# A hybrid decoder step on one core: the samples' state products turned on TensorE and summed in groups by VectorE

## The chip, the cores and the metric

The kernel runs on one core of a Trainium2 chip. The metric is the time of one launch on the device in microseconds (us); a time is compared as the median of several runs. The engines are named as in the profile: PE is TensorE's matrix multiplication and PEld its loading of stationary weights, DVE is VectorE, ACT is ScalarE, POOL is GpSimd, and SP is SyncE, which issues most DMAs.

## The reference, cut to what matters

One layer of a decoder is computed for a prompt of 16 learned + 256 tokens and for 8 samples of one token each. RMSNorm, a wide input projection, a short convolution branch, an mLSTM branch with 8 heads, an output projection, then a gated feed-forward part with a convolution, and a last RMSNorm. Model width is 2048, a head has 128 key and 256 value columns. For a sample the mLSTM step of one head is

```
c_new = carry * c_prev + g * k v^T          # 128 x 256 state per sample and head
num   = q . c_new                           # sum over the 128 key rows
den   = q . n_new
h     = num / max(|den|, exp(-m))
```

What is edited is the sum `q . c_new`: for each of the 8 samples, 256 numbers, each a sum over 128 key rows.

## The kernel before, in words

The activations lie with features on the 128 partitions and tokens along the free axis (prompt columns first, the 8 samples as the last 8 columns). All weights are streamed from memory once in units of 128 x 1024 float32. For each unit SP loads `w_raw` (a ring of 4), ACT rounds it to `w_hi` (L713), DVE subtracts to `w_lo` (L984), and PE runs three passes of 8 matmuls: `w_hi` with the high part of the activations (L1526), `w_hi` with their low part (L1530), `w_lo` with the high part (L1534). Two units make a strip, one 128-row block of outputs in one of four PSUM banks. PE takes the units in a fixed written order; before each unit it waits for `hi_done`, before the third pass for `lo_done`. DVE makes `w_lo` four units ahead: its `step(i)` in a head makes the low part of unit i + 4. The next load into a `w_raw` slot waits for the `w_lo` made from it, and ACT's next `w_hi` in a slot waits until PE has used the old one.

A head takes 32 units (strips 0 to 15). `front(n)` does strips 0 to 3 (q, k and two of v), `back(n)` the twelve others: u, c, b, g_a, o, g_b, twice. Between strips PE does the head's attention products in the four banks aux0 to aux3. After strip 10 (units 20 and 21) it runs one block (L1605 to L1636): the numerators into aux0 and aux1, columns 0 to 257 (PM = 258); the new prompt state into aux3; then the samples' part; then the denominators, `ones` times `p_hi` and `p_lo`, into aux2 (L1635, L1636).

The samples' part starts from `sacc[:, 0, :]`, 128 partitions x 256 columns, made by DVE at i = 15 to 18. A partition p = 8 g + b holds sample b and a group g of 8 key rows, whose 8 products are already added. What is left is the sum over the 16 groups g, and putting the 256 value columns on the partitions. Before, one matmul per 128 columns does both, with `sacc` stationary and the 0/1 matrix `sel` (128 x 8, made once at the start by a DVE reduction of the identity, L1021) moving; each leaves 128 x 8 in aux0, columns 258 to 273.

At i = 22 DVE forms the denominators (L1205, L1208), their reciprocal (L1212), the heads' outputs `h_t` for the prompt (L1215, L1217) and for the samples (L1220). POOL waits for all of `h_t` (`hs_step`, L627), multiplies by the gate (L628), adds the other branch (L631), then forms `cu` for the next half of the head (L589), for which DVE waits with its convolution (L1229).

A transpose on PE (`turn`, L1404) is a matmul with the identity; at the end of the kernel `turn_y` puts a pair of them, 128 x 128 float32 each, into aux0 and aux1 between two strips of the down projection (L1702, L1703, recorded under L1405).

Of the kernel before, what the change touches and what calls it, by code (L numbers as in the profile page):

```python
# [6 lines left out]
def hybrid_decoder_step(nc, ins, outs, scratch_rows, scratch_v, scratch_q):  # L7
# [11 lines left out]
    ALU, ACT = mybir.AluOpType, mybir.ActivationFunctionType  # L19
# [7 lines left out]
    P = 128  # L27
# [3 lines left out]
    NS = x_sample.shape[0]  # L31
# [13 lines left out]
    NM = NT - M0  # L45
    PM = TP - M0
# [57 lines left out]
    with ctx:  # L104
        def sb(name, shape, dt=f32):
            return ctx.enter_context(nc.sbuf_tensor(name, shape, dt))

        def sem(name):
            return ctx.enter_context(nc.semaphore(name))
# [12 lines left out]
        ident = sb("ident", [P, P])  # L122
# [13 lines left out]
        scn = sb("scn", [P, 2 * P + NS * H])  # L136
        a3 = sb("a3", [P, 3, H])
        scale_t = sb("scale_t", [P, NS])
        sel = sb("sel", [P, NS])


        base = (nc.sbuf_base + 223) // 512 * 512 + 288
# [4 lines left out]
        def at(name, shape, dt=f32):  # L147
            size = int(np.prod(shape[1:])) * 4
            size = (size + 31) // 32 * 32
            t = nc.alloc_sbuf_tensor_at(name, shape, dt, offset=base + cursor[0])  # L150
            cursor[0] += size
            assert cursor[0] <= REGION, (name, cursor[0])
            return t
# [10 lines left out]
        sacc = at("sacc", [P, 2, DV])  # L164
# [31 lines left out]
        h_t = at("h_t", [P, 2, NM])  # L196
# [99 lines left out]
        aux = [ctx.enter_context(nc.psum_tensor(f"aux{i}", [P, 512], f32)) for i in range(4)]  # L296
# [29 lines left out]
            sem("arg_done"), sem("exp_done"), sem("masked"), sem("g3_done"), sem("p_done"))  # L326
        scores_done, kv_turned, kv_done, vs_done, v_kept = (
            sem("scores_done"), sem("kv_turned"), sem("kv_done"), sem("vs_done"), sem("v_kept"))
        wsc_done, qkd_done, qkd_turned, sn_done, sel_done = (
            sem("wsc_done"), sem("qkd_done"), sem("qkd_turned"), sem("sn_done"), sem("sel_done"))  # L330
        psum_step, n_kept = sem("psum_step"), sem("n_kept")
        kv_split, p_kept, p_split, tail_split = sem("kv_split"), sem("p_kept"), sem("p_split"), sem("tail_split")
        sample_done, num_done, cn_done, pc_done = (
# [32 lines left out]
        def out_of(s):  # L366
            return s + 1 + RING
# [613 lines left out]
        def _(v):  # L981
# [25 lines left out]
            def newton(r, c, root, mean, out, done, d0):  # L1007
# [10 lines left out]
            v.sem_inc(evacuated, RING)  # L1018
            v.wait_ge(pads_clear, 3)
            v.wait_ge(const_done, 3)  # L1020
            v.tensor_reduce(sel[:, :], ident[:, :].rearrange("p (g b) -> p b g", b=NS), mybir.AxisListType.X, ALU.add)\  # L1021
             .then_inc(sel_done, 1)

            for k in range(KT):
                v.wait_ge(xh_done, k + 1)
# [100 lines left out]
            def back(n):  # L1126
# [6 lines left out]
                for i in range(8, HEAD_U):  # L1133
# [68 lines left out]
                    if i == 22:  # L1202

                        v.wait_ge(num_done, n + 1)
                        v.tensor_tensor(den[:, :], aux[2][:, 0:NM], rb[:, R_EM:R_EM + NM], ALU.max)\  # L1205
                         .then_inc(h_step, 1)
                        v.wait_ge(h_step, hs + 1)
                        v.scalar_tensor_tensor(out=den[:, :], in0=aux[2][:, 0:NM], scalar=-1.0, in1=den[:, :],  # L1208
                                               op0=ALU.mult, op1=ALU.max)\
                                                .then_inc(h_step, 1)  # L1210
                        v.wait_ge(h_step, hs + 2)
                        v.reciprocal(rden[:, :], den[:, :])\  # L1212
                         .then_inc(h_step, 1)
                        v.wait_ge(h_step, hs + 3)
                        v.tensor_tensor(h_t[:, 0, 0:PM], aux[0][:, 0:PM], rden[:, 0:PM], ALU.mult)\  # L1215
                         .then_inc(h_step, 1)
                        v.tensor_tensor(h_t[:, 1, 0:PM], aux[1][:, 0:PM], rden[:, 0:PM], ALU.mult)\  # L1217
                         .then_inc(h_step, 1)
                        v.wait_ge(sample_done, n + 1)
                        v.tensor_tensor(h_t[:, :, PM:NM], aux[0][:, PM:PM + 2 * NS].rearrange("p (a b) -> p a b", a=2),  # L1220
                                        rden[:, PM:NM].unsqueeze(1).broadcast_to([P, 2, NS]), ALU.mult)\
                         .then_inc(hs_step, 1)
                    for jj in range(2):
# [29 lines left out]
            with v.Fori(0, H - 1) as n:  # L1253
                back(n)
                front(n + 1)
            back(H - 1)

            def tile_of(t, m, a, b):
# [144 lines left out]
        def _(pe):  # L1403
            def turn(out, in_, k):  # L1404
                return pe.transpose(out, in_, ident[0:k, 0:k])  # L1405
# [150 lines left out]
            def mix_strip(n, s, c0, c1, between=None):  # L1556
                strip(n * 16 + s, n * HEAD_U + 2 * s, 2 * s, s % RING, xh, xl, c0, c1, (), between)
# [21 lines left out]
            def back(n):  # L1579
                for s in range(4, 16):  # L1580
                    mix_strip(n, s, C0, NT)
                    if s == 4:

                        pe.wait_ge(evacuated, out_of(n * 16 + 3))
                        for c0, k0, nr, q0, nq in ((0, 0, P, 0, PM), (W1, P, P, Q1, PM - Q1), (W2, 2 * P, T2, Q2, T2)):
                            keys = k_t[:, k0:k0 + nr] if k0 < 2 * P else tails[:, 0:T2]
                            mm = pe.matmul(aux[0][0:nr, c0:c0 + nq], keys, q_t[:, q0:q0 + nq],  # L1587
                                           start=True, stop=True)
                        mm.then_inc(scores_done, 1)

                        for t in range(2):
                            for w in range(2):
                                turn(aux[1][:, t * DV + w * P:t * DV + (w + 1) * P], v_t[:, w, t * P:(t + 1) * P], P)
                            turn(aux[2][:, t * P:(t + 1) * P], k_t[:, t * P:(t + 1) * P], P)
                        if n > 0:
                            pe.wait_ge(qkd_done, n * 3 + 3)
                        rows = P if n > 0 else Q4P
                        turn(aux[3][0:rows, 0:P], tails[:, 0:rows], P).then_inc(kv_turned, 1)
                    if s == 5 and n == 0:

                        pe.wait_ge(v_kept, n + 1)
                        pe.wait_ge(qkd_done, n * 3 + 3)
                        turn(aux[1][0:3 * NS, QC:QC + P], tails[:, Q4P:Q4P + 3 * NS], P)\
                            .then_inc(qkd_turned, 1)
                    if s == 10:  # L1605

                        pe.wait_ge(tail_split, n * 3 + 3)
                        pe.wait_ge(p_split, n + 1)
                        pe.wait_ge(kv_split, n + 1)
                        pe.wait_ge(vs_done, n * 2 + 2)  # L1610
                        for a in range(2):
                            va = slice(a * P, (a + 1) * P)
                            pe.matmul(aux[a][:, 0:PM], v_hi[:, 0, va], p_main[:, 0:W1], start=True, stop=False)
                            pe.matmul(aux[a][:, 0:PM], v_hi[:, 0, va], p_rest[:, 0:W1], start=False, stop=False)  # L1614
                            pe.matmul(aux[a][:, Q2:PM], v_hi[0:TK, 2, va], p_tail[0:TK, :], start=False, stop=False)
                            pe.matmul(aux[a][:, 0:PM], v_lo[:, 0, va], p_main[:, 0:W1], start=False, stop=False)  # L1616
                            pe.matmul(aux[a][:, Q1:PM], v_1[:, va], pt[:, W1:W2], start=False, stop=True)  # L1617

                        state = aux[3][:, 0:DV + 2]
                        for t in range(2):  # L1620
                            pe.matmul(state, k_hi[:, t, :], v_hi[:, t, :], start=(t == 0), stop=False)  # L1621
                            pe.matmul(state, k_hi[:, t, :], v_lo[:, t, :], start=False, stop=False)  # L1622
                            pe.matmul(state, k_lo[:, t, :], v_hi[:, t, :], start=False, stop=False)
                        mm = pe.matmul(state, k_hi[0:TK, 2, :], v_hi[0:TK, 2, :], start=False, stop=True)
                        mm.then_inc(cn_done, 1)

                        pe.wait_ge(sel_done, 1)
                        pe.wait_ge(sacc_step, (n + 1) * (JG + 1))
                        for w in range(2):
                            mm = pe.matmul(aux[0][:, PM + w * NS:PM + (w + 1) * NS], sacc[:, 0, w * P:(w + 1) * P],  # L1630
                                           sel[:, :], start=True, stop=True)
                        mm.then_inc(sample_done, 1)

                        pe.wait_ge(psum_step, n * PST + PST)
                        pe.matmul(aux[2][:, 0:NM], ones[:, :].bitcast(f32r), p_hi[:, :], start=True, stop=False)  # L1635
                        pe.matmul(aux[2][:, 0:NM], ones[:, :].bitcast(f32r), p_lo[:, :], start=False, stop=True)\  # L1636
                          .then_inc(num_done, 1)
# [126 lines left out]
```

## Time and profile before

| | us |
|---|---|
| median of 3 runs (lowest, highest) | 1701.0 (1700.27, 1701.26) |
| the profiled execution, whole | 1700.78 |
| its span, first to last instruction | 1699.0 |
| PE busy in the span | 1688.1 (99%) |
| DVE busy | 1194.5 (70%) |
| ACT busy | 766.9 (45%) |
| POOL busy | 479.8 (28%) |
| mean granted TensorE clock | 0.998 of full speed |

The profiled execution is 0.2 us under the median, and 1.8 us of it lie outside the span. In the rows below a line of a timeline has start, length, engine, line, operation, output <- inputs, shape and count; consecutive equal instructions are merged, and a bracket at the end tells how long the engine was idle before and what released it. Matmuls overlap in such rows: one starts some 0.12 us after the one before it and lasts 0.28 us, so that what one costs PE is the distance from start to start.

### The profile page before, as it was taken

How to read it: one execution, taken by the hardware profiler on the slowest of the kernel's cores; microseconds unless marked ns; L12 is line 12 of the kernel's file. 1: busy time of each engine (PE TensorE's matmuls, PEld its weight loads, DVE VectorE, ACT ScalarE, POOL GpSimd, SP SyncE). 2: the span in 40 equal slices, each digit the busy share in tenths (PEclk: the TensorE clock that was granted, in tenths of full speed). 3: DMA queues.
4: the chain of work that ended last, by engine and by line, in shares of the span. 5: the costliest groups of instructions: out<-in, count | busy, mean ns of one | idle time of the engine just before them, and what ended most of it. 6: DMA issues, size and time to landing. Idle time of an engine off the chain costs nothing.

```text
span 1699.0 us, 37193 instructions
## 1 busy us (share of the span) xinstructions
PE 1688.1 (99%) x13726; PEld 1682.0 (99%) x13726; DVE 1194.5 (70%) x1901; ACT 766.9 (45%) x916; POOL 479.8 (28%) x501
## 2 busy tenths in 40 slices
PE   9999999999999999999999999999999999999997
PEld 8999999999999999999999999999999999999997
DVE  5875857677585767758688877877455777777554
ACT  6545435353443535344444554544333434334443
POOL 4432414242241524224333222221000222222220
PEclk9999999999999999999999999999999999999999
DMA  8788786878778687787766666656666666666663
GB/s 204 192 222 199 197 212 168 216 177 219 192 190 216 166 216 179 212 194 195 193 177 186 189 175 184 185 173 176 183 181 182 182 179 179 179 179 178 183 176 120
DMA packets 591165, 318.80 MB, mean 188 GB/s; under 512 B 17684, under 2 KB 585988, under 8 KB 588988
## 3 DMA queue, kind: packets, MB, share of 16 engines
q1 hardware_dynamic: 578564, 292.99, 63.8%
q10 hardware_dynamic: 10448, 21.57, 5.0%
q0 software_dynamic: 2064, 2.92, 0.8%
q8 instruction: 72, 1.18, 0.3%
q14 instruction: 17, 0.14, 0.0%
HBM read 305.09 MB, written 12.78 MB: 187 GB/s over the span
## 4 chain that ended last, share of the span: by engine, by line
PE 99%; ACT 0%; POOL 0%; DVE 0%; issue 0%; ACTq 0%; POOLq 0%; DVEq 0%
PE strip L1526 32%; PE strip L1530 32%; PE strip L1534 32%; PE aux L1405 1%; PE aux L1413 1%; PE strip L1457 0%; PE aux L1587 0%; PE aux L1477 0%; PE strip L1470 0%; PE aux L1617 0%; PE aux L1616 0%; PE aux L1630 0%; PE strip L1405 0%; PE aux L1621 0%; PE aux L1622 0%; PE aux L1614 0%
## 5 line engine op out<-in xcount | busy, mean ns | idle before, releaser
L713 ACT ACTIVATE w_hi<-w_raw 128x1024 fp32r<-128x1024 f32 x557 | 588.6, 1060 | 787.7 <-PE strip L1534 755.9
L984 DVE TENSOR_TENSOR w_lo<-w_raw,w_hi 128x1024 fp32r<-128x1024 f32 x556 | 708.7, 1278 | 296.5 <-ACT w_hi L713 295.8
L1526 PE MATMUL strip<-xh,w_hi 128*128 128x268 f32 (+1 forms) x2016 | 290.9, 286 | 0.0
L1530 PE MATMUL strip<-xl,w_hi 128*128 128x268 f32 (+1 forms) x2016 | 290.0, 286 | 0.0
L1534 PE MATMUL strip<-xh,w_lo 128*128 128x268 f32 (+1 forms) x2016 | 290.0, 286 | 0.0
L1526 PEld LDWEIGHTS strip<-xh,w_hi 128*128 128x128 f32 x2016 | 265.1, 188 | 0.2
L1534 PEld LDWEIGHTS strip<-xh,w_lo 128*128 128x128 f32 x2016 | 265.2, 188 | 0.0
L1530 PEld LDWEIGHTS strip<-xl,w_hi 128*128 128x128 f32 x2016 | 265.2, 188 | 0.0
L1526 PE MATMUL strip<-x2h,w_hi 128*128 128x266 f32 x1408 | 200.1, 284 | 0.0
L1530 PE MATMUL strip<-x2l,w_hi 128*128 128x266 f32 x1408 | 199.9, 284 | 0.0
L1534 PE MATMUL strip<-x2h,w_lo 128*128 128x266 f32 x1408 | 199.9, 284 | 0.0
L1526 PEld LDWEIGHTS strip<-x2h,w_hi 128*128 128x128 f32 x1408 | 183.2, 189 | 0.1
L1534 PEld LDWEIGHTS strip<-x2h,w_lo 128*128 128x128 f32 x1408 | 183.2, 189 | 0.0
L1530 PEld LDWEIGHTS strip<-x2l,w_hi 128*128 128x128 f32 x1408 | 183.1, 189 | 0.0
L684 POOL TENSOR_TENSOR gg<-sg,cz 128x264 f32<-128x264 f32 x44 | 57.9, 1317 | 409.2 <-ACT sg L929 409.2
L687 POOL TENSOR_TENSOR hid<-gg,cz 128x264 f32<-128x264 f32 x44 | 73.6, 1674 | 101.7 <-DVE cz L1333 101.7
L1526 PE MATMUL strip<-hh,w_hi 128*128 128x264 f32 x704 | 102.2, 286 | 0.0
L1534 PE MATMUL strip<-hh,w_lo 128*128 128x264 f32 x704 | 101.3, 285 | 0.0
L1530 PE MATMUL strip<-hl,w_hi 128*128 128x264 f32 x704 | 101.2, 284 | 0.0
L1534 PEld LDWEIGHTS strip<-hh,w_lo 128*128 128x128 f32 x704 | 92.2, 189 | 0.0
L1530 PEld LDWEIGHTS strip<-hl,w_hi 128*128 128x128 f32 x704 | 91.9, 188 | 0.0
L1526 PEld LDWEIGHTS strip<-hh,w_hi 128*128 128x128 f32 x704 | 91.7, 188 | 0.0
(330 smaller groups left out, 1534.4 us busy)
## 6 DMA issues: line engine op xcount, KB each, us to landing
w_raw<-in_w_in SPq DMA_DIRECT2D x256, 512.0 KB, 4.5
w_raw<-in_w_up SPq DMA_DIRECT2D x176, 512.0 KB, 4.1
w_raw<-in_w_down SPq DMA_DIRECT2D x64, 512.0 KB, 4.0
w_raw<-in_w_out SPq DMA_DIRECT2D x32, 512.0 KB, 4.5
w_raw<-in_w_down SPq DMA_DIRECT2D x32, 384.0 KB, 3.4
out<-c_st ACTq DMA_DIRECT2D x8, 1024.0 KB, 7.0
c_st<-in_state_mlstm_C ACTq DMA_DIRECT2D x7, 1024.0 KB, 10.4
rb<-scratch_rows ACTq DMA_DIRECT2D x8, 270.0 KB, 5.3
```

The lines of the kernel that those rows point to most:

```text
L684: g.tensor_tensor(gg[:, :], sg[:, :], cz[:, 0, :], ALU.mult).then_inc(gg_done, 1)
L687: g.tensor_tensor(hid[:, :], gg[:, :], cz[:, 1, :], ALU.mult).then_inc(hid_done, 1)
L713: act.activation(w_hi[:, slot, :], w_raw[:, slot, :], ACT.Copy).then_inc(hi_done, 1)
L984: v.tensor_tensor(w_lo[:, slot, :], w_raw[:, slot, :], w_hi[:, slot, :].bitcast(f32), ALU.subtract).then_inc(lo_done, 1)
L1405: return pe.transpose(out, in_, ident[0:k, 0:k])
L1413: pe.matmul(aux[1][:, 0:NM], ones[:, :], acc[:, :], start=True, stop=True)
L1526: pe.matmul(bank[b][:, 0:c1 - c0], w_hi[:, slot, w], rh[:, k0 + k, c0:c1], start=(first and k == 0), stop=False)
L1530: pe.matmul(bank[b][:, 0:c1 - c0], w_hi[:, slot, w], rl[:, k0 + k, c0:c1], start=False, stop=False)
L1534: mm = pe.matmul(bank[b][:, 0:c1 - c0], w_lo[:, slot, w], rh[:, k0 + k, c0:c1], start=False, stop=(last and k == kk - 1))
```

## The change

The two matmuls with `sel` become two transposes of `sacc[:, 0, 0:128]` and `sacc[:, 0, 128:256]`, the first into aux0 and the second into aux1, columns 258 to 385. DVE then sums each over the 16 groups with a reduction (`hsum`, 128 x 8 each), waits for its own two results, and multiplies them by the reciprocal as before. `sel`, its making at the start and PE's wait for it go. DVE's first wait for POOL's clearing of three tiles now stands before its first `xl` instead. The attention weights of a head (`pt`, L1142 to L1149) are formed ahead of that unit's low part in both kernels; the diff does not touch them.

```
-        sel = sb("sel", [P, NS])
+        hsum = sb("hsum", [P, 2, NS])
...
             v.wait_ge(const_done, 3)
-            v.tensor_reduce(sel[:, :], ident[:, :].rearrange("p (g b) -> p b g", b=NS), mybir.AxisListType.X, ALU.add)\
-             .then_inc(sel_done, 1)
...
                         v.wait_ge(sample_done, n + 1)
-                        v.tensor_tensor(h_t[:, :, PM:NM], aux[0][:, PM:PM + 2 * NS].rearrange("p (a b) -> p a b", a=2),
+                        for w in range(2):
+                            v.tensor_reduce(hsum[:, w, :], aux[w][:, PM:PM + P].rearrange("p (g b) -> p b g", b=NS),
+                                            mybir.AxisListType.X, ALU.add).then_inc(hsum_done, 1)
+                        v.wait_ge(hsum_done, n * 2 + 2)
+                        v.tensor_tensor(h_t[:, :, PM:NM], hsum[:, :, :],
                                         rden[:, PM:NM].unsqueeze(1).broadcast_to([P, 2, NS]), ALU.mult)\
                          .then_inc(hs_step, 1)
...
-                        pe.wait_ge(sel_done, 1)
                         pe.wait_ge(sacc_step, (n + 1) * (JG + 1))
                         for w in range(2):
-                            mm = pe.matmul(aux[0][:, PM + w * NS:PM + (w + 1) * NS], sacc[:, 0, w * P:(w + 1) * P],
-                                           sel[:, :], start=True, stop=True)
+                            mm = turn(aux[w][:, PM:PM + P], sacc[:, 0, w * P:(w + 1) * P], P)
                         mm.then_inc(sample_done, 1)
```

`hsum` takes 32 bytes of a partition more than `sel` did; every other tile keeps its address.

On PE, in the block after strip 10 of the first head, these instructions stood in a row before (names are output <- moving, stationary; `p_hi` and `p_lo` are the denominators' parts):

```order
L1623 MATMUL aux<-v_hi,k_lo 128x258
L1624 MATMUL aux<-v_hi,k_hi 128x258
L1630 MATMUL aux<-sel,sacc 128x8 [waits sacc_step,sel_done]
L1630 MATMUL aux<-sel,sacc 128x8
L1635 MATMUL aux<-p_hi,ones 128x266 [waits psum_step]
L1636 MATMUL aux<-p_lo,ones 128x266
L1526 MATMUL strip<-xh,w_hi 128x268 [waits hi_done]
```

In the same place of the changed kernel stand these (line numbers have moved by two; L1407 is `turn`):

```order
L1625 MATMUL aux<-v_hi,k_lo 128x258
L1626 MATMUL aux<-v_hi,k_hi 128x258
L1407 MATMUL aux<-ident,sacc 128x128 [waits sacc_step]
L1407 MATMUL aux<-ident,sacc 128x128
L1635 MATMUL aux<-p_hi,ones 128x266 [waits psum_step]
L1636 MATMUL aux<-p_lo,ones 128x266
L1528 MATMUL strip<-xh,w_hi 128x268 [waits hi_done]
```

Two instructions are exchanged for two, one wait is gone, and nothing else on PE changes its place.

On DVE, at i = 22 and 23 of the first head, the row before was this (`rden` is the reciprocal, `cgs` the next strip's result):

```order
L1212 RECIPROCAL rden<-den 128x266 [waits h_step]
L1214 REGISTER_ALU
L1215 TENSOR_TENSOR h_t<-aux,rden 128x258 [waits h_step]
L1217 TENSOR_TENSOR h_t<-aux,rden 128x258
L1220 TENSOR_TENSOR h_t<-aux,rden 128x2x8 [waits sample_done]
L992 REGISTER_ALU
L993 TENSOR_TENSOR cgs<-strip,rbc 128x268 [waits unit_used]
L984 TENSOR_TENSOR w_lo<-w_raw,w_hi 128x1024 [waits hi_done]
```

In the changed kernel it is this:

```order
L1210 RECIPROCAL rden<-den 128x266 [waits h_step]
L1212 REGISTER_ALU
L1213 TENSOR_TENSOR h_t<-aux,rden 128x258 [waits h_step]
L1215 TENSOR_TENSOR h_t<-aux,rden 128x258
L1219 TENSOR_REDUCE hsum<-aux 128x8 [waits sample_done]
L1219 TENSOR_REDUCE hsum<-aux 128x8
L1222 TENSOR_TENSOR h_t<-hsum,rden 128x2x8 [waits hsum_done]
L992 REGISTER_ALU
L993 TENSOR_TENSOR cgs<-strip,rbc 128x268 [waits unit_used]
L984 TENSOR_TENSOR w_lo<-w_raw,w_hi 128x1024 [waits hi_done]
```

Two reductions and a wait come in between the prompt's outputs and the samples', ahead of `cgs` and the next low part. The order of ACT, POOL and SP is the same in both.

## Rows read from the trace of the kernel before

**Rows 1.** The page: busy time by engine; the chain that ended last, by engine.
```profile
PE 1688.1 (99%) x13726; PEld 1682.0 (99%) x13726; DVE 1194.5 (70%) x1901; ACT 766.9 (45%) x916; POOL 479.8 (28%) x501
...
PE 99%; ACT 0%; POOL 0%; DVE 0%; issue 0%; ACTq 0%; POOLq 0%; DVEq 0%
```

**Rows 2.** All waits of PE: engine, line, for whom, us in total, times, longest.
```profile
PE aux L1413 <- POOL b_row L483: 2.1, 1, 2.1
PE aux L1729 <- DVE rfs L1015: 1.1, 1, 1.1
```

**Rows 3.** Busy time in stretches (length, engines, granted clock, DMA): PE alone.
```profile
40.00:815.00 775.00, 775.00 (x6276) 1.00 0.78 198
...
85.00:104.00 19.00, 19.00 (x158) 1.00 0.81 219
1572.00:1690.00 118.00, 117.89 (x973) 1.00 0.55 153
```

**Rows 4.** Timeline of PE in head 0, the end of the block.
```profile
93.16 0.28 PE L1623 MATMUL aux<-v_hi,k_lo 128*128 128x258 f32 x1
93.28 0.28 PE L1624 MATMUL aux<-v_hi,k_hi 80*128 80x258 f32 x1
93.40 0.51 PE L1630 MATMUL aux<-sel,sacc 128*128 128x8 f32 x4
93.76 0.37 PE L1635 MATMUL aux<-p_hi,ones 128*128 128x266 f32 x1
93.97 0.29 PE L1636 MATMUL aux<-p_lo,ones 128*128 128x266 f32 x1
94.10 0.65 PE L1526 MATMUL strip<-xh,w_hi 128*128 128x268 f32 x4
```

**Rows 5.** Timeline of PE, a pair of turns between strips of the down projection.
```profile
1572.12 0.28 PE L1534 MATMUL strip<-hh,w_lo 128*128 128x264 f32 x1
1572.24 0.38 PE L1405 MATMUL aux<-ident,xg 128*128 128x128 f32 x2
1572.38 0.74 PE L1526 MATMUL strip<-hh,w_hi 128*128 128x264 f32 x4
...
1572.59 0.65 PE L1526 MATMUL strip<-hh,w_hi 128*128 128x264 f32 x4
```

**Rows 6.** Instructions of L1630 and L1405: ns min/median/max, first and last start.
```profile
L1630 PE MATMUL aux<-sel,sacc x32: 172/256/256, 93.4 to 790.4; 128*128 128x8 f32 x32
...
L1405 PE MATMUL aux<-ident,xg x32: 270/271/307, 1572.2 to 1689.5; 128*128 128x128 f32 x32
```

**Rows 7.** Timeline of DVE: the start of the kernel, then head 0.
```profile
2.83 0.38 DVE L1021 TENSOR_REDUCE sel<-ident 128x8 f32<-128x128 f32 x1 [2.83 <-POOL tails L488]
...
91.69 0.43 DVE L1196 TENSOR_TENSOR sacc<-sacc 128x256 f32<-128x256 f32 x1
...
99.52 0.43 DVE L1205 TENSOR_TENSOR den<-aux,rb 128x266 f32<-128x266 f32 x1
99.98 0.43 DVE L1208 SCALAR_TENSOR_TENSOR den<-aux,den 128x266 f32<-128x266 f32 x1
...
102.98 0.17 DVE L1220 TENSOR_TENSOR h_t<-aux,rden 128x16 f32<-128x16 f32 x1
103.06 0.43 DVE L993 TENSOR_TENSOR cgs<-strip,rbc 128x268 f32<-128x268 f32 x1
103.41 1.76 DVE L984 TENSOR_TENSOR w_lo<-w_raw,w_hi 128x1024 fp32r<-128x1024 f32 x1
...
107.64 0.36 DVE L1229 TENSOR_SCALAR cv<-cu,vecs 128x266 f32<-128x266 f32 x1 [0.78 <-POOL cu L589]
...
108.91 1.22 DVE L984 TENSOR_TENSOR w_lo<-w_raw,w_hi 128x1024 fp32r<-128x1024 f32 x1
```

**Rows 8.** Timeline of POOL in head 0.
```profile
103.32 0.77 POOL L628 TENSOR_TENSOR so<-so,h_t 128x266 f32<-128x266 f32 x1 [9.11 <-DVE h_t L1220]
...
105.74 1.75 POOL L589 TENSOR_TENSOR cu<-us,cgs 128x268 f32<-128x268 f32 x1
```

**Rows 9.** Timeline of PE in head 0, unit 27: its first and third pass.
```profile
108.75 1.14 PE L1526 MATMUL strip<-xh,w_hi 128*128 128x268 f32 x8
...
110.70 1.14 PE L1534 MATMUL strip<-xh,w_lo 128*128 128x268 f32 x8
```

**Rows 10.** Loads of `w_raw`: count, size, us to landing; ACT's timeline in head 0.
```profile
w_raw<-in_w_in SPq DMA_DIRECT2D x256, 512.0 KB, 4.5
...
111.94 1.06 ACT L713 ACTIVATE w_hi<-w_raw 128x1024 fp32r<-128x1024 f32 x1 [1.86 <-PE strip L1534]
```

More of the change, by code:

```diff
@@ L328, in hybrid_decoder_step @@
             sem("scores_done"), sem("kv_turned"), sem("kv_done"), sem("vs_done"), sem("v_kept"))
-        wsc_done, qkd_done, qkd_turned, sn_done, sel_done = (
-            sem("wsc_done"), sem("qkd_done"), sem("qkd_turned"), sem("sn_done"), sem("sel_done"))
+        wsc_done, qkd_done, qkd_turned, sn_done, hsum_done = (
+            sem("wsc_done"), sem("qkd_done"), sem("qkd_turned"), sem("sn_done"), sem("hsum_done"))
         psum_step, n_kept = sem("psum_step"), sem("n_kept")
```

## The prediction

> **What bounds the kernel now.** I read the page first: PE is busy for 1688.1 of the span's 1699.0 us, and the chain that ended last is PE at 99%, every other engine at 0% [rows 1]. A share of the whole can hide a stage in which PE waits, so the next view is PE's waits. The list has two entries, 2.1 us for a clearing at the start and 1.1 us in the last ten microseconds [rows 2]; from 40 to 815 us, where all eight heads lie, PE is busy 775.00 of 775.00 us at a granted clock of 1.00, the 2.4 GHz level [rows 3]. So in the edited stage the time is the sum of PE's distances from start to start. An edit there counts in full if it shortens or lengthens PE's own row, and for nothing if it is on DVE, unless DVE becomes so late that PE has to wait.
>
> **PE's term.** Before, the samples' sums were four matmul records a head: 16 instructions, 32 records [rows 6], two to each float32 matmul, each with its own weight load. In head 0 the last state matmul starts at 93.28 and the second denominator matmul at 93.97 [rows 4]. Between these two starts lie the four records and the first denominator matmul: 0.69 us. Its size shows a second cost: L1635 to L1636 takes 0.21 us, where its neighbours of like width are 0.12 us apart (93.16 to 93.28). I read the additional 0.09 as the price of going from plain float32 operands back to the rounded kind.
>
> The trace has what will stand there in the changed kernel, at another place: two float32 turns of 128 x 128 between two rows of rounded matmuls. The last strip matmul starts at 1572.12, the turns at 1572.24, the next strip at 1572.38, and its second matmul at 1572.59 [rows 5]: 0.47 us over the same sequence (matmul, the float32 pair, first rounded matmul, second rounded matmul), with the same 0.21 at the return. The widths of the rounded matmuls, 264 there and 258 and 266 here, are the same for this purpose, and the granted clock is 1.00 in both stretches [rows 3].
>
> So a head's block changes by 0.47 - 0.69 = -0.22 us, and eight heads by 8 x -0.22 = -1.8 us. Bounds from the nearest rows: turns that cost PE nothing would leave only two ordinary distances of 0.12 out of the 0.69, so -0.45 us a head and -3.6 us in all. On the other side is the turn's recorded length, 0.27 us [rows 6], taken as time that nothing overlaps: 0.12 + 2 x 0.27 + 0.21 = 0.87 us, which is +0.18 a head and +1.4 us in all. I take the pair of rows 5, since it is the same pair, in form and in surroundings.
>
> At this place a page speaks against the change. The Trainium skill, "TensorE: Matmul & The Clock Gate", Part 4: PE-mode transpose, gives some 275 ns for one transpose within a kernel and 390 ns alone. The rows agree with 275 as a length (0.270 to 0.273) and show that it isn't what the row pays: both turns and their return lie in 0.47 us. By 275 ns apiece the sum would be near the upper bound, an estimate from that page; by the distances it is -1.8 us.
>
> The wait for `sel_done` goes; it was met at 3.2 us [rows 7], 90 us before its first use, and is worth nothing. The wait for `sacc` stays: DVE ends it at 92.12 [rows 7] and the first product is at 93.40 [rows 4], 1.2 us of room, and the turn starts no earlier in the row than that product did.
>
> **DVE's term.** The reduction at the start (0.38 us) goes. It started at 2.83 us, and DVE next waits for ACT's first rounded activations in any case: nothing. In each head come two reductions of 128 x 128 out of PSUM, and a wait on DVE's own result. This form isn't in the trace. The reduction out of SBUF with the same stride took 0.38 us. From below, two elementwise operations out of PSUM, 266 columns in 0.43 and 16 in 0.17 [rows 7], give (0.43 - 0.17) / 250 = 1.04 ns a column, so 0.17 + 112 x 0.00104 = 0.29 us for 128. For the wait, L1208 starts 0.03 after the end of L1205, on which it waits, while unconnected operations start 0.09 before the one ahead has ended (102.98 + 0.17 against 103.06): some 0.1 us. Together 0.6 to 0.9 us a head; I take 0.8, near the reduction, since it is the same operation.
>
> What is queued behind it on DVE: the evacuation `cgs` (103.06) and the low part at 103.41, then, through POOL, `so` at 103.32 and `cu` at 105.74 [rows 8], for which DVE waits at 107.64, and the low part at 108.91 [rows 7]. All come up to 0.8 us later. Who needs them:
> - The low part at 103.41 is for unit 27 and is ready at 105.17. Unit 27 begins on PE at 108.75, and its third pass, the first to read it, at 110.70 [rows 9]: 5.5 us of room. The one at 108.91 is for unit 29, which comes two units later, of 2.93 us each (unit 22 starts at 94.10 in rows 4, five before unit 27), so its third pass is at 116.56, 6.4 us after it is ready.
> - The bank that `cgs` empties is asked for three strips on, at PE's third matmul of unit 29, about 114.9 us: 11 us of room.
> - The load into the slot of that low part starts at 105.17 and lands 4.5 us later, near 109.7; ACT takes the slot at 111.94, after PE has released it [rows 10]: 2.2 us of room.
>
> With 0.8 us against room of 2.2 us and more, DVE's term is hidden and costs nothing. If the cover were gone, it would be 8 x 0.8 = +6.4 us. In each head DVE catches up before the next one: it still waits 0.78 us for POOL at 107.64 and for ACT's rounding after that.
>
> **The sum.** The profiled execution took 1700.78 us, its span and 1.78 around it. -1.8 gives 1699.0; the median of before lies 0.2 above that execution, so a median of 1699.2 us, 0.1% under 1701.0. What a measurement of this kernel can tell from no change is about 0.2%, 3.4 us: below 1697.6 is faster, above 1704.4 slower.
>
> **Rivals.**
> - *A turn holds PE for its recorded length.* For it: 0.27 us in every row of turns [rows 6], and a first turn that, unlike that of rows 5, follows a matmul over 80 rows. Against it: the starts in rows 5. It gives the upper bound, +1.4, thus 1702.4 us.
> - *The gain is given back or never arrives.* PE's next wait could end later by what it saved, or the products' cost had been hidden under their neighbours' weight loads. For it: the block's weight loads are as long as its matmuls are apart. Against it: in rows 4 and 5 both blocks run up to the next strip without a pause. It gives 1701.0 us.
> - *DVE's addition reaches PE: the slower side.* One mechanism: the reductions push the low part of unit 27 past the moment PE asks for it. It decides from the point where DVE's addition is over 5.5 us, or 2.7 us for each reduction; at seven times the row that this rests on, the strided read out of PSUM would have to be far slower than that out of SBUF. Each 0.1 us beyond costs 0.8 us in eight heads. With a reduction of 3.2 us, the addition is 6.5, 1 us a head shows, and the time is 1699.2 + 8 = 1707 us. For it speaks only that no row has a reduction out of PSUM.
> - *More than the pair shows.* The first matmul after the turns pays no 0.09, or the turns go under the neighbours: the lower bound, -3.6, thus 1697.4 us, the only way past 0.2% that PE's rows offer.
>
> **How the numbers follow.** The forecast, 1699.2 us, has a chance of 0.78 (its own range 1698.4 to 1700.0, from 0.5 us of scatter between runs before and 0.03 us a head in reading the distances). A turn at full length 0.05, the gain given back 0.08, DVE's delay 0.04, more than the pair 0.05. Only the last, with a little of the scatter, is faster by over 0.2%: 0.06. Only DVE's delay, and what I haven't thought of on that side, is slower by over 0.2%: 0.05. The rest is within: 0.89. The range reaches from the middle between the forecast and the lower bound, 1698.0, to 1701.2, no change and its scatter, and leaves out about 1 to 2 in 10.
>
> **What the changed profile would show.** If PE's term is right, the state matmul of each head stands 0.47 us ahead of the second denominator matmul, the two turns are 0.11 us apart, and PE has no new entry among its waits. If DVE's term is right, the reductions take 0.29 to 0.38 us each, the samples' `h_t` starts 0.6 to 0.9 us later after the prompt's than before, POOL's `so` moves by as much, and the low part of unit 27 is still over 4 us early. A distance of 0.69 or more, or a PE wait for a low part between 90 and 815 us, would make the prediction wrong.

## The result, and the profile after

The changed kernel takes 1707.5 us (median of 6 runs, 1707.1 to 1708.5), the kernel before, in 6 runs, 1700.8 us. The ratio is 1.0041, with a 95% interval of 1.0029 to 1.0053: slower by 0.4%. The forecast was 1699.2 us, with a range of 1698.0 to 1701.2 and no change as the likeliest; the time lies outside, on the other side.

The page of the changed kernel gives busy times and the chain that ended last as [rows 1] do:

```profile
PE 1694.1 (99%) x13710; PEld 1688.4 (99%) x13710; DVE 1197.3 (70%) x1916; ACT 767.9 (45%) x916; POOL 479.1 (28%) x501
...
PE 99%; ACT 0%; POOL 0%; issue 0%; DVE 0%; ACTq 0%; POOLq 0%; DVEq 0%
```

PE's waits (engine, line, for whom, us in total, times, longest) are the same two as in [rows 2]:

```profile
PE aux L1415 <- POOL a L484: 2.1, 1, 2.1
PE aux L1729 <- DVE rfs L1015: 1.4, 1, 1.4
```

So the 6.7 us aren't a wait; the second entry is 0.3 us longer, no more. PE has 16 matmuls fewer, is busy 6 us longer, and in the heads its granted clock is 1.00 as before. The heads' stretch, PE alone:

```profile
40.00:815.00 775.00, 775.00 (x6207) 1.00 0.78 196
```

In the same 775 us stand 6207 matmul records where 6276 stood [rows 3]. Of the 69 that are missing the edit takes 16; the others are lost to a slower pace.

The block itself did what was forecast. The timeline of PE in head 0 of the changed kernel, to be laid beside [rows 4]:

```profile
92.48 0.29 PE L1626 MATMUL aux<-v_hi,k_hi 80*128 80x258 f32 x1
92.60 0.38 PE L1407 MATMUL aux<-ident,sacc 128*128 128x128 f32 x2
92.74 0.37 PE L1635 MATMUL aux<-p_hi,ones 128*128 128x266 f32 x1
92.95 0.28 PE L1636 MATMUL aux<-p_lo,ones 128*128 128x266 f32 x1
```

From 92.48 to 92.95 it is 0.47 us, against 0.69 before. What is longer are the passes of 8 matmuls behind the block, of which nothing was edited. The timeline of PE in head 0 of the changed kernel, where [rows 9] stand in the kernel before:

```profile
106.97 1.15 PE L1536 MATMUL strip<-xh,w_lo 128*128 128x268 f32 x8
107.96 1.16 PE L1528 MATMUL strip<-xh,w_hi 128*128 128x268 f32 x8
108.95 1.16 PE L1532 MATMUL strip<-xl,w_hi 128*128 128x268 f32 x8
109.94 1.15 PE L1536 MATMUL strip<-xh,w_lo 128*128 128x268 f32 x8
110.94 1.16 PE L1528 MATMUL strip<-xh,w_hi 128*128 128x268 f32 x8
```

From 106.97 to 110.94 there are four passes in 3.97 us (3.973 in the trace's nanoseconds), 0.993 each, 124.2 ns a matmul. In [rows 9] it is 1.95 us for two (1.953), 0.977 each, 122.1 ns a matmul. The kernel before has both lengths: the timeline of its head 0 ahead of the block, and of head 1 behind it:

```profile
88.14 1.16 PE L1526 MATMUL strip<-xh,w_hi 128*128 128x268 f32 x8
89.13 1.15 PE L1530 MATMUL strip<-xl,w_hi 128*128 128x268 f32 x8
...
200.47 1.14 PE L1530 MATMUL strip<-xl,w_hi 128*128 128x268 f32 x8
201.45 1.14 PE L1534 MATMUL strip<-xh,w_lo 128*128 128x268 f32 x8
202.43 1.14 PE L1526 MATMUL strip<-xh,w_hi 128*128 128x268 f32 x8
```

0.99 us ahead of the block in head 0, 0.98 behind it and in the heads that follow. I call them the slow and the quick rhythm. Heads are counted from 0, and a head's block stands behind its strip 10. From one block to the next there are 12 strips of 268 columns with 6 passes each that were seen in either rhythm: strips 11 to 15 and the next head's strip 0 behind the edited block, and strips 5 to 10 behind the attention block that stands after strip 4. In the kernel before all 72 passes are quick from the first block on, in the changed kernel all 72 are slow: 72 x 0.0165 = 1.2 us a head. Strip 4 also has 268 columns; it is slow in both kernels. The distance from block to block shows the sum: the first denominator matmul of head 1 in the kernel before, whose forerunner stands in [rows 4] at 93.76,

```profile
193.30 0.37 PE L1635 MATMUL aux<-p_hi,ones 128*128 128x266 f32 x1
```

and in the changed kernel, 92.74 above:

```profile
193.22 0.37 PE L1635 MATMUL aux<-p_hi,ones 128*128 128x266 f32 x1
```

99.54 us became 100.48: +0.94 a head. In the trace that is +1.19 in the 72 passes, -0.22 in the block, and -0.03 in small shifts beside it. Seven such distances make 6.5 of the 6.7 us. (The first block itself starts anywhere from 92.7 to 94.1 us in the profiles of this document, so heads are compared by their distances.)

DVE's part, in the timeline of head 0 of the changed kernel (compare [rows 7]):

```profile
101.66 0.42 DVE L1215 TENSOR_TENSOR h_t<-aux,rden 128x258 f32<-128x258 f32 x1
102.00 0.48 DVE L1219 TENSOR_REDUCE hsum<-aux 128x8 f32<-128x128 f32 x2
102.51 0.18 DVE L1222 TENSOR_TENSOR h_t<-hsum,rden 128x16 f32<-128x16 f32 x1
```

The prompt's second half in the kernel before, ahead of the samples' `h_t` at 102.98 in [rows 7]:

```profile
102.65 0.42 DVE L1217 TENSOR_TENSOR h_t<-aux,rden 128x258 f32<-128x258 f32 x1
```

All 16 reductions took 0.28 us, and the samples' `h_t` starts 0.85 us after the prompt's second half, against 0.33 before. Nothing of it reaches PE, whose waits are the two above.

### The profile page after: what moved, and what is told of

It is laid out like the page before. It is cut to its first block, busy times and chain, and to the rows that moved or that the text cites. A ratio compares the mean times of both kernels' runs of the same rounds, so it can differ in the third digit from the quotient of the medians.

```text
span 1705.4 us, 37168 instructions
## 1 busy us (share of the span) xinstructions
PE 1694.1 (99%) x13710; PEld 1688.4 (99%) x13710; DVE 1197.3 (70%) x1916; ACT 767.9 (45%) x916; POOL 479.1 (28%) x501
## 4 chain that ended last, share of the span: by engine, by line
PE 99%; ACT 0%; POOL 0%; issue 0%; DVE 0%; ACTq 0%; POOLq 0%; DVEq 0%
PE strip L1528 32%; PE strip L1536 32%; PE strip L1532 32%; PE aux L1407 1%; PE aux L1415 0%; PE strip L1459 0%; PE aux L1589 0%; PE aux L1479 0%; PE strip L1472 0%; PE aux L1619 0%; PE aux L1618 0%; PE strip L1407 0%; PE aux L1623 0%; PE aux L1616 0%; PE aux L1624 0%; PE aux L1625 0%
```

## The experiments

Three theories were open. A: the rhythm is PE's own, and the block with the turns leaves PE in the slow one. B: DVE's reductions slow PE. C: it hangs on the number of instructions in PE's row, which lost a wait in each head. Times stand beside those of the kernel before on the same chip. Where nothing else is said, the lines show strips behind the block of head 1, just under 210 us; what is said of the strips behind the attention block is read from the same traces.

**The turns without the reductions.** DVE's old line is put back.

```
-                        for w in range(2):
-                            v.tensor_reduce(hsum[:, w, :], aux[w][:, PM:PM + P].rearrange("p (g b) -> p b g", b=NS), ...)
-                        v.wait_ge(hsum_done, n * 2 + 2)
-                        v.tensor_tensor(h_t[:, :, PM:NM], hsum[:, :, :],
+                        v.tensor_tensor(h_t[:, :, PM:NM], aux[0][:, PM:PM + 2 * NS].rearrange("p (a b) -> p a b", a=2),
```

> The changed kernel's PE (the two turns), but DVE as before: the two reductions and their wait are left out, and the samples' h_t is made from the first 16 turned columns, so the samples' sums are not formed. Theory A (PE's own rhythm: after the block with the turns the 268-column matmuls of a head follow each other every 124.1 ns, after the block with the products every 122.0 ns): the time stays at that of the changed kernel, 1707 us, and the passes of 8 after the block last 0.993 us. Theory B (the reductions out of PSUM, or the delay they make, slow PE): the time falls to the forecast, 1699 us, and the passes last 0.976 us. Theory C (one instruction less in each head's PE row, the dropped wait): 1707 us, as A.

Measured: 1707.7 us against 1700.7, ratio 1.0038 (1.0018 to 1.0058). PE's timeline:

```profile
206.69 1.15 PE L1524 MATMUL strip<-xh,w_hi 128*128 128x268 f32 x8
207.68 1.16 PE L1528 MATMUL strip<-xl,w_hi 128*128 128x268 f32 x8
208.67 1.16 PE L1532 MATMUL strip<-xh,w_lo 128*128 128x268 f32 x8
```

0.99 us a pass without any reduction, behind the attention block too: B falls.

**The products with reductions.**

```
+        hsum = sb("hsum", [P, 2, NS])
...
+                        for w in range(2):
+                            v.tensor_reduce(hsum[:, w, :], aux[w][:, 0:P].rearrange("p (g b) -> p b g", b=NS),
+                                            mybir.AxisListType.X, ALU.add).then_inc(hsum_done, 1)
+                        v.wait_ge(hsum_done, n * 2 + 2)
                         v.tensor_tensor(h_t[:, :, PM:NM], aux[0][:, PM:PM + 2 * NS].rearrange("p (a b) -> p a b", a=2),
```

> The kernel before with its products by sel on PE, and two reductions of 128 x 128 out of the same two banks added on DVE ahead of the samples' h_t, with a wait for them; their results are not used. Theory A: 1700.8 us, as before, passes of 8 at 0.976 us, since PE's row is that of before. Theory B: 1707 us or more, passes of 0.993 us. Theory C: 1700.8 us.

Measured: 1700.6 us against 1700.7, ratio 1.0000 (0.9988 to 1.0011). PE's timeline:

```profile
206.84 1.14 PE L1540 MATMUL strip<-xh,w_lo 128*128 128x268 f32 x8
207.82 1.14 PE L1532 MATMUL strip<-xh,w_hi 128*128 128x268 f32 x8
208.79 1.14 PE L1536 MATMUL strip<-xl,w_hi 128*128 128x268 f32 x8
```

Quick passes. DVE's term is nothing, as costed.

**Neither products nor turns.**

```
-                        pe.wait_ge(sacc_step, (n + 1) * (JG + 1))
-                        for w in range(2):
-                            mm = turn(aux[w][:, PM:PM + P], sacc[:, 0, w * P:(w + 1) * P], P)
-                        mm.then_inc(sample_done, 1)
...
-                        v.wait_ge(sample_done, n + 1)
+                        v.wait_ge(sacc_step, (n + 1) * (JG + 1))
```

> Neither products nor turns: the samples' part of the block is left out on PE, and h_t of the samples is made from columns that hold something else, without reductions. By distances alone a head's block is 0.45 us shorter than before: 1697.2 us if the passes after it last 0.976 us as before. Theory A has to be seen in the passes: if it takes the products to bring PE into the quicker rhythm, they last 0.993 us and the time is 1697.2 + 8 x 1.1 = 1706 us; if it is the turns that bring it into the slower one, 1697.2. Theory B: 1697.2 us. Theory C (the wait is gone here too): 1706 us.

Measured: 1697.1 us against 1700.7, ratio 0.9978 (0.9967 to 0.9989). PE's timeline:

```profile
207.39 1.14 PE L1524 MATMUL strip<-xh,w_hi 128*128 128x268 f32 x8
208.37 1.14 PE L1528 MATMUL strip<-xl,w_hi 128*128 128x268 f32 x8
```

Quick passes: the products aren't needed for them. The sum by distances comes out to 0.1 us where the rhythm stays the same, so the counting was sound and the rhythm is the missing term. This kernel has dropped the wait too and is quick, which speaks against C.

**The turns with a second wait.**

```
+                        pe.wait_ge(x_kept, KT // 2)
                         pe.wait_ge(sacc_step, (n + 1) * (JG + 1))
```

> The changed kernel, with a second wait ahead of the turns, for a semaphore that has long been reached (x_kept), in the place of the wait for sel that was dropped; PE's row then has as many wait instructions as before. Theory A: 1707 us, passes of 0.993 us. Theory B: 1707 us. Theory C: the passes return to 0.976 us and the time falls to 1699 us.

Measured: 1707.4 us against 1700.7, ratio 1.0040 (1.0025 to 1.0056). PE's timeline behind the block of head 1:

```profile
207.50 1.16 PE L1536 MATMUL strip<-xh,w_lo 128*128 128x268 f32 x8
208.49 1.15 PE L1528 MATMUL strip<-xh,w_hi 128*128 128x268 f32 x8
```

Putting a wait back doesn't bring the quick passes back: C falls in that form. A is left, but something new shows at the attention block, which no version of the kernel edits. Two passes ahead of it (strip 4) and two behind it, first in head 1, then in head 2:

```profile
151.95 1.15 PE L1532 MATMUL strip<-xl,w_hi 128*128 128x268 f32 x8
152.94 1.15 PE L1536 MATMUL strip<-xh,w_lo 128*128 128x268 f32 x8
...
156.66 1.14 PE L1532 MATMUL strip<-xl,w_hi 128*128 128x268 f32 x8
157.63 1.14 PE L1536 MATMUL strip<-xh,w_lo 128*128 128x268 f32 x8
...
251.84 1.16 PE L1532 MATMUL strip<-xl,w_hi 128*128 128x268 f32 x8
252.84 1.15 PE L1536 MATMUL strip<-xh,w_lo 128*128 128x268 f32 x8
...
256.56 1.16 PE L1532 MATMUL strip<-xl,w_hi 128*128 128x268 f32 x8
257.55 1.15 PE L1536 MATMUL strip<-xh,w_lo 128*128 128x268 f32 x8
```

The same instructions, entered from slow passes both times, leave the quick rhythm in head 1 and the slow one in head 2 and after. In the trace's nanoseconds the two heads keep step: from a dozen matmuls behind the edited block to the attention block, 60 us, PE's starts lie at the same distances to within 1 ns. The first to differ is the second transpose of the attention block, which starts 3 ns later in head 2.

That was no part of A as a property of the turns. So A was split in two: A1, the rhythm follows from the exact distances ahead of it, whatever instructions make them; A2, turns in this block leave the slow one.

**The turns ahead of the state, and last in the block.** The same lines in two other places of the block.

```
+                        pe.wait_ge(sacc_step, (n + 1) * (JG + 1))       # first version: here
+                        for w in range(2):
+                            mm = turn(aux[w][:, PM:PM + P], sacc[:, 0, w * P:(w + 1) * P], P)
+                        mm.then_inc(sample_done, 1)
                         state = aux[3][:, 0:DV + 2]
...
                         pe.matmul(aux[2][:, 0:NM], ones[:, :].bitcast(f32r), p_lo[:, :], start=False, stop=True)\
                           .then_inc(num_done, 1)
+                        ...                                             # second version: the same four lines here
```

> The changed kernel with its two turns (and their wait) ahead of the matmuls of the prompt's state instead of behind them; the same instructions otherwise. Theory A1 (two steady rhythms of the 268-column passes exist, 0.977 and 0.993 us for 8 matmuls, and which of them PE falls into hangs on the exact distances in the block ahead, so that a shift can change it): the sum of the block stays the same, and the passes after it may be of either length; 1699 us if they are the quick ones. Theory A2 (a pair of plain float32 turns anywhere in this block leaves PE in the slow rhythm): passes of 0.993 us, 1707 us.

> The changed kernel with its two turns (and their wait) behind the denominators, last in the block, right ahead of the next strip, as the turns of the down projection stand. Theory A1: either rhythm; 1699 us with the quick one; if both this and the version with the turns ahead of the state are slow, A1 has lost what speaks for it. Theory A2: passes of 0.993 us, 1707 us.

Measured: ahead of the state 1699.6 us (8 runs, 1698.8 to 1700.0) against 1700.7, ratio 0.9993 (0.9982 to 1.0004); last in the block 1704.1, ratio 1.0020 (1.0009 to 1.0032). PE's timeline with the turns ahead of the state:

```profile
207.38 1.14 PE L1536 MATMUL strip<-xh,w_lo 128*128 128x268 f32 x8
208.35 1.14 PE L1528 MATMUL strip<-xh,w_hi 128*128 128x268 f32 x8
```

and with the turns last in the block:

```profile
207.56 1.16 PE L1536 MATMUL strip<-xh,w_lo 128*128 128x268 f32 x8
208.56 1.15 PE L1528 MATMUL strip<-xh,w_hi 128*128 128x268 f32 x8
```

The first is quick with the same two turns, behind both blocks: A2 falls. It is the forecast made good, 0.4 us above the 1699.2, by moving four lines, and 7.9 us below the changed kernel; its blocks stand 99.33 us apart, 0.21 less than before, where -0.22 was forecast. That it also beats the kernel before is not shown, since the interval holds 1. The second is slow behind the edited block and quick behind the attention block, so its distance of 99.91 us, and its time, lie between the two.

**266 columns for eight strips.** Edited in the changed kernel and in the kernel before.

```
-                    mix_strip(n, s, C0, NT)
+                    mix_strip(n, s, C0 if s in (4, 5, 10, 11) else M0, NT)
...
-                        take(u0 + i, i // 2 % RING, out[:, :], c0, width)
+                        take(u0 + i, i // 2 % RING, out[:, :], c0, width, c0)
```

> The changed kernel; eight of the twelve strips of a head's second part (b, g_a, o, g_b, twice) are run over 266 instead of 268 columns: their first two columns were never read. Theory A1 and A2 alike have the two rhythms from the trace at 268 columns alone: the output projection, with 266, runs at 0.973 us a pass in both kernels, also right after slow passes. So the eight strips run at 0.973 to 0.974: 8 x 8 heads x 6 passes x 0.019 = 7.3 us less than the changed kernel, 1700.2 us with the four strips of 268 columns still slow; down to 1697 us if those are quick too. If the slowness were not bound to the width (Theory D: the turns cost PE something that the following passes pay in any form), the eight strips would still take 0.99 and the time would be 1706 us.

> The kernel before with the same eight strips over 266 columns. Its passes are already quick, 0.977 against 0.973 to 0.974: 8 x 8 x 6 x 0.003 = 1.2 us less, and in head 0, where strips 6 to 10 run at 0.993, another 0.5: 1699.1 us under A1 and A2. If a narrower strip shifts the quick rhythm of the four wide ones into the slow one (A1 allows it): 4 strips x 6 x 8 x 0.016 = 3.1 us more, 1702 us.

Measured: 1703.6 us (ratio 1.0015, 1.0004 to 1.0027) and 1704.0 us (1.0022, 1.0010 to 1.0033). PE's timeline of the first, in the narrowed strips:

```profile
207.75 1.15 PE L1536 MATMUL strip<-xh,w_lo 128*128 128x266 f32 x8
208.73 1.15 PE L1528 MATMUL strip<-xh,w_hi 128*128 128x266 f32 x8
```

Both expectations missed. A pass over 266 columns takes 0.987 us here, in either kernel, while the output projection of the kernel before does 266 columns in 0.973. Width alone doesn't set the length of a pass. One thing that differs is where the moving rows lie (here they begin at column 14 of rows of 280, there at column 4 of rows of 272); rows of another length were not tried in the heads. That this is the cause is not shown: 0.987 may as well be the slow rhythm of a pass of 266 columns, and 0.973 its quick one. The kernel before became slower because its passes went from 0.977 to 0.987: 8 x 8 x 6 x 0.010 = 3.8 us, against 3.3 measured.

**The products last in the block, and ahead of the state.** No turns at all, the products of the kernel before in the two other places. What was left against A1 was A3: only turns leave the slow rhythm, where no long enough row of other matmuls undoes it.

```
-                        pe.wait_ge(sel_done, 1)
-                        pe.wait_ge(sacc_step, (n + 1) * (JG + 1))
-                        for w in range(2):
-                            mm = pe.matmul(aux[0][:, PM + w * NS:PM + (w + 1) * NS], ...
-                        mm.then_inc(sample_done, 1)
...
                           .then_inc(num_done, 1)
+                        ...                              # the same lines here (or ahead of the state)
```

> The kernel before, its products by sel (and their waits) moved behind the denominators, last in the block; no turns. Theory A3 (only turns leave PE in the slow rhythm, and only where no row of other matmuls long enough to undo it follows before the strip; products never do): passes of 0.977 us after the block, 1700.7 us. Theory A1 (the rhythm follows from the distances in the block, whatever instruction makes them): either rhythm is possible with products too; passes of 0.993 us after the block, as with the turns in this place, would be 1700.7 + 3 to 7 = 1704 to 1708 us and would refute A3.

> The kernel before, its products by sel (and their waits) moved ahead of the state's matmuls. Theory A3: passes of 0.977 us, 1700.7 us. Theory A1: either rhythm; slow passes would give 1704 to 1708 us and refute A3, quick ones leave both open.

Measured: last 1705.3 us against 1701.0, ratio 1.0026 (1.0013 to 1.0038); ahead of the state 1701.2, ratio 1.0002 (0.9991 to 1.0013). PE's timeline with the products last:

```profile
207.70 1.16 PE L1530 MATMUL strip<-xl,w_hi 128*128 128x268 f32 x8
208.69 1.15 PE L1534 MATMUL strip<-xh,w_lo 128*128 128x268 f32 x8
```

Slow passes behind the block without one turn of `sacc`: A3 falls. Those behind the attention block are quick; with the products ahead of the state both are.

**The turns where they are, behind a reordered state.**

```
+                        pe.matmul(state, k_hi[0:TK, 2, :], v_hi[0:TK, 2, :], start=True, stop=False)
                         for t in range(2):
...
-                        mm = pe.matmul(state, k_hi[0:TK, 2, :], v_hi[0:TK, 2, :], start=False, stop=True)
```

> The changed kernel with its turns where they are; of the seven matmuls of the prompt's state ahead of them the last one, over 80 rows, now comes first. Nothing is added or left out. Theory A3: the turns still stand right ahead of the denominators: passes of 0.993 us, 1707 us. Theory A1: the distances ahead of the turns shift by some ns, so quick passes are possible; 1699 us would refute A3, 1707 leaves both open.

Measured: 1703.5 us against 1701.0, ratio 1.0017 (1.0006 to 1.0028). Neither number; the timeline of PE says why. Two passes ahead of the edited block and two behind it, first in head 0, then in head 1:

```profile
89.42 1.15 PE L1532 MATMUL strip<-xl,w_hi 128*128 128x268 f32 x8
90.41 1.15 PE L1536 MATMUL strip<-xh,w_lo 128*128 128x268 f32 x8
...
95.15 1.14 PE L1532 MATMUL strip<-xl,w_hi 128*128 128x268 f32 x8
96.13 1.14 PE L1536 MATMUL strip<-xh,w_lo 128*128 128x268 f32 x8
...
188.78 1.14 PE L1532 MATMUL strip<-xl,w_hi 128*128 128x268 f32 x8
189.76 1.14 PE L1536 MATMUL strip<-xh,w_lo 128*128 128x268 f32 x8
...
194.47 1.16 PE L1532 MATMUL strip<-xl,w_hi 128*128 128x268 f32 x8
195.47 1.16 PE L1536 MATMUL strip<-xh,w_lo 128*128 128x268 f32 x8
```

The same instructions in the same order leave the quick rhythm in head 0 and the slow one in head 1 and all heads after it. What differs is how PE came to them: in head 0 from slow passes, in the others from quick ones. So the block's instructions alone don't decide; the state in which they find PE counts too. A1 allows that, but this run doesn't show that the distances carry the state. With slow passes behind the edited block alone, the time again lies between the two.

The number of instructions is out as well: the changed kernel, its two versions with the turns moved, and this one have the same instructions on PE in four orders, and take 1707.5, 1699.6, 1704.1 and 1703.5 us.

## Why the prediction was wrong

- *What bounds the kernel*: right. PE's row is the time, before and after.
- *PE's term*: the block changed by 0.47 - 0.69 = -0.22 us in every head, as taken from the turns of the down projection. Turns held PE for their distance, not their recorded length. The 0.09 us for the return from plain float32 is borne out too: with neither products nor turns the two denominator matmuls stood 0.13 us apart, not 0.21.
- *The step that failed*: "the time is the sum of PE's distances from start to start", with an edit's part read off its own block. The sum holds, but the distances of the unedited passes were taken as fixed, a term put at nothing without a reason. 72 of them a head went from 0.977 to 0.993 us, +1.19 us a head, five times the block's gain. None of the rivals had that: the one in which the gain is given back stopped at zero, and the slower one was DVE. That DVE's rival names 1707 us as an example is chance: it needed reductions of 3.2 us and a PE wait for a low part, and there were neither. Nor did a sign of being wrong appear: the block was 0.47 us and PE had no new wait, so the signs named didn't cover the way in which it failed.
- *DVE's term*: hidden, as costed, and a little smaller than bounded: 0.28 us a reduction against 0.29 to 0.38, 0.52 us of delay against 0.6 to 0.9. Reductions added to the old kernel left the time where it was.
- *The range*: the middle between the forecast and the lower bound is (1699.2 + 1697.4) / 2 = 1698.3, not 1698.0; the measured time is outside either way.
- The kernel before had shown it. In its head 0 the same 268-column pass takes 0.99 us ahead of the block and 0.98 behind it, at one granted clock and without a wait. The prediction compared distances of different instructions and never those of one instruction in two stretches, and took its pace from rows behind the block alone.

The Trainium skill, "TensorE: Matmul & The Clock Gate", Back-to-back issue gap, says that in a stream of weight loads and matmuls both set the spacing, and gives one gap for a width. The rows differ from the one gap: one width has two, 122.1 and 124.2 ns for 268 columns, at the same granted clock. No run here shows the part of the weight loads in them.

What stays open is what chooses between them. The runs show that moving instructions in a block can switch the rhythm, and that neither DVE's reductions, nor the number of PE's instructions, nor the turns as such decide it. They also show that what PE has visibly just been through isn't enough: in the run with the second wait two heads keep step to 1 ns for 60 us and then part. A1 could still hold with differences finer than the trace's nanosecond or with a longer memory; neither was tested. That PE's reads meet those of another engine or the landing of a DMA was tested only as far as DVE's reductions go.

## What to carry to other kernels

Where one engine is busy all the time with thousands of equal instructions, compare the spacing of one instruction form in several stretches before believing a gain of less than a percent: here 2 ns a matmul outweighed the edit five times. A small edit in such a row can switch the spacing of what follows, even behind a block that it doesn't touch, so give a forecast of it that risk on the slower side, and try the same edit one place earlier or later before dropping it: four lines moved took back all of the 6.7 us. A gain over the kernel before is not shown.

## What the runs showed of the hardware that was not expected

Matmuls of 268 columns with alternating weight loads ran in one of two steady spacings here, 122.1 or 124.2 ns, over tens of microseconds without a wait and at a granted clock of 1.00, and a block of a dozen or two other matmuls between them switched it either way or kept it. Two heads whose starts kept step to 1 ns for 60 us still left the same block in different rhythms. A narrower matmul wasn't always quicker: 266 columns beginning at column 14 took 123.4 ns each (0.987 us for 8), more than 268 beginning at column 12 in the quick rhythm; the reason is not shown.
